# A trunk step with product-key experts on one core: every expert slot handled alone, long work cut into even pieces, six then nine row buffers

## The reference, cut to what matters

```python
def one(hb):                                        # hb: 128 tokens x 1024
    q = (hb @ w_pq).reshape(t, 8, 2, 128)
    sc = jnp.einsum('thpd,hpkd->thpk', q, keys)     # 128 keys per half
    sv, si = lax.top_k(sc, 16)
    cand = sv[:, :, 0, :, None] + sv[:, :, 1, None, :]
    cidx = si[:, :, 0, :, None] * 128 + si[:, :, 1, None, :]
    cv, ci = lax.top_k(cand, 16)
    eidx = take_along_axis(cidx, ci)                # 8 heads x 16 experts per token
    gate = softmax(cv)
    act = gelu(einsum('thkd,td->thk', u_tab[eidx], hb))
    return einsum('thk,thkd->td', gate * act, v_tab[eidx])
```

## Time and profile before

| | us |
|---|---|
| median of 3 runs | 7569.1 (7564.6 to 7570.45) |
| profiled execution, its own time | 7554.87 |
| its span, first to last instruction | 7553.1 |
| PE busy | 4377.6 (58%) |
| DVE busy | 3105.2 (41%) |
| ACT busy | 1460.9 (19%) |
| POOL busy | 1477.2 (20%) |

### The profile page before, as it was taken

How to read it: one execution, slowest core, us unless ns; L and a number is a source line. 1 busy time by engine, 2 the same in 40 slices (tenths; PEclk the granted TensorE clock), 3 DMA queues, 4 the chain that set the end, 5 groups by cost and what they waited for, 6 DMA issues and landing times.

```text
span 7553.1 us, 59355 instructions
## 1 busy us (share of the span) xinstructions
PE 4377.6 (58%) x18966; PEld 1902.7 (25%) x18966; DVE 3105.2 (41%) x7579; ACT 1460.9 (19%) x4806; POOL 1477.2 (20%) x1454
## 2 busy tenths in 40 slices
PE   7999726555553256355579996366545523454455
PEld 2576412222221011111135854022212200111111
DVE  1531462223334354645445215522233344555454
ACT  0142011111111122222222421111111111222222
POOL 0200011111111123234322000111111111333333
PEclk9999857877775577767789998677877756766777
DMA  5102335554554489799941023355555445888998
GB/s 191 55 13 85 133 132 198 201 208 181 191 193 165 178 317 384 282 366 358 363 160 55 1 112 130 142 200 205 202 189 186 182 151 204 327 339 308 361 359 326
DMA packets 222742, 1573.73 MB, mean 208 GB/s; under 512 B 25648, under 2 KB 27312, under 8 KB 35040
## 3 DMA queue, kind: packets, MB, share of 16 engines
q0 software_dynamic: 184320, 1342.26, 47.0%
q1 hardware_dynamic: 38112, 227.68, 8.0%
HBM read 1566.56 MB, written 3.28 MB: 208 GB/s over the span
## 4 chain that ended last, share of the span: by engine, by line
PE 37%; DMA 33%; DVE 14%; ACT 6%; issue 6%; POOL 2%; DVEq 1%; ACTq 0%; SPq 0%; POOLq 0%
DMA arena<-in_experts,arena 31%; PE ps L920 16%; PE ps L704 8%; DVE sq L1374 7%; ACT arena L1061 3%; PE ps L825 2%; ACT arena L1054 2%; PE ps L848 2%; POOL arena L682 2%; DMA arena<-in_weights 2%; PE ps L721 2%; PE ps L870 1%; PE ps L838 1%; PE ps L894 1%; ACT arena L1050 1%
## 5 line engine op out<-in xcount | busy, mean ns | idle before, releaser
L920 PE MATMUL ps<-arena 64*64 64x512 f32 x10240 | 1974.6, 902 | 2843.9 <-ACT arena L1061 2842.5
L1374 DVE CUSTOM_DVE_ANT_0 sq<-arena 128x1024 f32<-128x1024 f32 x1280 | 1568.6, 1225 | 2904.2 <-DMA arena<-in_experts,arena 2875.6
L682 POOL DMA_INDIRECT arena<-in_experts,arena x1280 | 1341.2, 1048 | 5500.4 <-PE ps L920 4283.4
L920 PEld LDWEIGHTS ps<-arena 64*64 64x64 f32 x10240 | 516.4, 186 | 4146.4 <-issue 4145.0
L1050 ACT ACTIVATE arena<-arena 128x2 f32<-128x2 f32 x640 | 130.2, 203 | 4670.5 <-DVE arena L1374 4670.5
L704 PE MATMUL ps<-arena 128*128 128x512 f32 (+3 forms) x1920 | 776.6, 561 | 25.7 <-DMA arena<-in_weights 23.8
L704 PEld LDWEIGHTS ps<-arena 128*128 128x128 f32 x1920 | 369.1, 195 | 432.1 <-issue 383.5
L1054 ACT ACTIVATE arena<-arena 128x1 f32<-128x1 f32 x1280 | 425.5, 379 | 46.3 <-issue 2.4
L1061 ACT ACTIVATE arena<-ident,arena 128x128 f32<-128x128 f32 x1280 | 433.3, 385 | 0.0
L894 PE MATMUL ps<-arena 128*128 128x256 f32 (+1 forms) x1024 | 321.1, 471 | 79.3 <-ACT arena L1026 62.0
L1267 DVE TENSOR_REDUCE negm<-ps 128x1 f32<-128x768 f32 (+4 forms) x160 | 119.0, 745 | 381.2 <-PE ps L831 214.8
(11 more groups left out here) (148 smaller groups left out, 3182.0 us busy)
## 6 DMA issues: line engine op xcount, KB each, us to landing
arena<-in_weights SPq DMA_DIRECT2D x182, 1024.0 KB, 6.8
arena<-in_experts,arena POOLq DMA_INDIRECT x1280, 7.9
arena<-mod_rows SPq DMA_DIRECT2D x24, 512.0 KB, 8.7
arena<-in_weights SPq DMA_DIRECT2D x8, 576.0 KB, 4.7
arena<-in_weights SPq DMA_DIRECT2D x4, 768.0 KB, 4.8
arena<-in_weights SPq DMA_DIRECT2D x6, 512.0 KB, 4.7
x<-in_x_sample SPq DMA_DIRECT2D x4, 512.0 KB, 11.3
arena<-in_g_norm SPq DMA_DIRECT2D x4, 512.0 KB, 11.0
```

Source lines behind the costliest of these rows:

```text
L682: pool.indirect_dma_start(out=ring[BUF[n]], out_offset=None, in_=ins["experts"], in_offset=bass.IndirectOffsetOnAxis(ap=index[n // SLOTS % ...
L920: last = MM(acc[h][to:to + 64, c * 512:(c + 1) * 512], diag[(n + odd) % 4][lo:lo + 64, lo:lo + 64], ring[BUF[n + odd]][lo:lo + 64, D + c * ...
L1374: V.tensor_tensor_reduce(out=sq[:], in0=ring[BUF[n]][:, 0:D], in1=h2_of_slot(n), scale=1.0, scalar=0.0, op0=ALU.mult, op1=ALU.add, accum_o ...
```

## The change

- Slots go one at a time: item `E` is one dot product on DVE; `Ea` is all of ACT's part (one gelu activation, times gate, diagonal), with no return to DVE; `Emm` is the four matmuls of one slot. The slot's gate carries no factor 0.5 now.
- The order is made by `Line`: slot s has its dot at place s, `Ea` at s + 0.4 and `Emm` at s + 1.6; other items are spread by cost over ranges of slots. `g`, `o` and `pq` are cut into 4 pieces, `p` into 2, `tk1` into one per tile, `tk2` into 6 (`tkx` and `tkg` once per tile, except tile 0).
- Buffers: five for the first 20 slots of a layer, six up to slot 259, nine for the last 380. One of them is `front`, where gains, mask and rope lie; SP reloads these for layer 1 after slot 636 of layer 0, and layer 1's `scale1`/`shift1` rows stand behind them in SP's queue.

```diff
-    return [("tk2", l, t, u), ("tkx", l, t, u), ("tkg", l, t, u)]
+    s = [("tk2", l, t, u, j) for j in range(6)]
+    return s + ([("tkx", l, t, u), ("tkg", l, t, u)] if alone else [])
...
+def pieces(items):
+    s = []
+    for i in items:
+        n = {"g": 4, "o": 4, "p": 2, "pq": 4}.get(i[0], 1)
+        s += [("part", i, j, n) for j in range(n - 1)] + [i]
+    return s
...
+    def slots(self, l):
+        n = l * NT * SLOTS
+        for s in range(NT * SLOTS):
+            self.put(s, [("E", n + s)])
+            self.put(s + .4, [("Ea", n + s)])
+            self.put(s + LAG, [("Emm", n + s)])
...
+        line.spread(-2, 16, pieces(r[at:]))
+        line.spread(20, 110, choose(l, 1))
+        line.spread(16, 232, pieces(merge(l, 1) + route(l, 1)))
+        line.spread(232, 250, choose(l, 2))
+        line.spread(262, 330, choose(l, 3))
+        if l == 0:
+            line.spread(300, 560, mod_items(1))
+        line.spread(390, 460, choose(l, 4))
...
-NBUF = 8
+NBUF = 9
...
+for _l in range(L):
+    BUF += [s % 5 for s in range(20)]
+    BUF += [s % 6 for s in range(236)]
+    BUF += [(s + 2) % 6 for s in range(4)]
+    BUF += [(s + 6) % 9 for s in range(380)]
...
                     if l:
-                        sp.wait_ge(*ready("oT", 0, NT - 1, 1))
-                        sp.wait_ge(*ready("qcN", 0, NT - 1))
-                        sp.wait_ge(ob_ready, NT)
-                    sp.dma_start(gains[:], to_all(row("gains", l))).then_inc(consts_in, 16)
+                        sp.wait_ge(slot_used, FINAL_IN[0, 4] + 1)
+                        sp.dma_start(mask, ins["mask"]).then_inc(masks_in, 16)
+                        sp.dma_start(rope, ins["rope"]).then_inc(masks_in, 16)
+                    sp.dma_start(gains, to_all(row("gains", l))).then_inc(consts_in, 16)
...
                     for c in range(2):
-                        for odd in range(2):
-                            for h in range(2):
-                                lo, to = 64 * h, 64 * (h ^ odd)
-                                last = MM(acc[h][to:to + 64, c * 512:(c + 1) * 512], diag[(n + odd) % 4][lo:lo + 64, lo:lo + 64],
-                                          ring[BUF[n + odd]][lo:lo + 64, D + c * 512:D + (c + 1) * 512], start=s == 0, stop=s == SLOTS - 2)
-                    last.then_inc(slot_used, 2)
+                        for h in range(2):
+                            lo, to = 64 * h, 64 * (h ^ (n % 2))
+                            last = MM(acc[h][to:to + 64, c * 512:(c + 1) * 512], diag[n % 4][lo:lo + 64, lo:lo + 64],
+                                      ring[BUF[n]][lo:lo + 64, D + c * 512:D + (c + 1) * 512], start=s < 2, stop=s >= SLOTS - 2)
+                    last.then_inc(slot_used, 1)
...
+                elif kind == "Ea":
+                    n = item[1]
+                    c, s = n % 16, n % SLOTS
+                    act.wait_ge(dot_done, n + 1)
+                    A(gel[:, c:c + 1], dots[:, c:c + 1], ACT.Gelu_apprx_tanh)
+                    act.drain()
+                    A(wts[:, c:c + 1], gel[:, c:c + 1], ACT.Copy, scale=gate[n // SLOTS % 2][:, s:s + 1])
+                    act.drain()
+                    if n >= 4:
+                        act.wait_ge(slot_used, n - 3)
+                    A(diag[n % 4], ident[:], ACT.Copy, scale=wts[:, c:c + 1]).then_inc(diag_done, 1)
```

More of the change, by code:

```diff
@@ L181, in mod_items @@
     return s
-GRP = 2
-NGRP = SLOTS // GRP
 ETILES = [(l, t) for l in range(L) for t in range(NT)]
-def tensor_cost(item):
-    k = item[0]
[L192 to L197, removed]
-    def __init__(self):
[L202 to L252, removed]
@@ L256, with cost @@
-SEAM = 6
+def pieces(items):
[4 more added lines that the diff above has]
+    return s
+def cost(item):
+    k = item[0]
+    if k == "part":
+        k, n = item[1][0], len(GROUPS[item[1][2]]) if item[1][0] == "pq" else 1
+    else:
+        n = len(GROUPS[item[2]]) if k in ("pq", "sc") else 1
+    return {"mod": 7.0, "hT2": 1.2, "g": 1.76, "p": 1.76, "mT": 1.2, "o": 1.76, "pq": .5 * n, "sc": .25 * n,
+            "n2": 3.0, "tk2": 1.5, "tk1": 1.0}.get(k, 0.1)
@@ new lines, with put, spread, items @@
+class Line:
+    def __init__(self):
+        self.points = []
+    def put(self, at, items):
+        self.points += [(at, i) for i in items]
+    def spread(self, a, b, items):
+        total = sum(cost(i) for i in items)
+        at = 0.0
+        for i in items:
+            at += cost(i)
+            self.points.append((a + (b - a) * at / total, i))
+    def slots(self, l):
[4 more added lines that the diff above has]
+            self.put(s + LAG, [("Emm", n + s)])
+        for t in range(NT):
+            end = (t + 1) * SLOTS - 1 + LAG
+            self.put(end + .1, [("ea", l, t), ("ex", l, t)])
+            after = [("sw", l, t, 0), ("sw", l, t, 1), ("ew", l, t)] + ([("g2", l, 1)] if t == 0 else []) + ([("y", t)] if l == L - 1 else [])
+            self.put(end + 2.1, after)
+    def items(self):
+        return [i for _, i in sorted(self.points, key=lambda p: p[0])]
@@ L412 @@
     if _e >= 2:
-        assert PLACE[("tk2", _l, _t, 0)] > PLACE[("Emm", NGRP * (_e - 1) - 1)]
-    for _u in range(4):
-        assert PLACE[("tkg", _l, _t, _u)] < PLACE[("E", NGRP * _e + 16 * _u)]
+        assert PLACE[("tk2", _l, _t, 0, 0)] > PLACE[("Emm", SLOTS * (_e - 1) - 1)]
+    assert PLACE[("tkg", _l, _t, 0)] < PLACE[("E", SLOTS * _e)]
+    if _t == 0:
+        for _u in range(4):
+            assert PLACE[("tkg", _l, _t, _u)] < PLACE[("E", SLOTS * _e + 32 * _u)]
 def build(nc, ins, outs):
@@ L510, in build @@
         esum = take(8)
-        dots, dsq, dlin, dth, dgate, wts = (take(8) for _ in range(6))
+        dots, gel, wts = (take(16) for _ in range(3))
         assert _e[0] <= R0 + 22928
@@ L699, in weight, with project @@
                 return block_in(b)
-            def project(dst, lhs, blocks, cols):
-                for k in range(DK):
+            def project(dst, lhs, blocks, cols, steps):
+                for k in steps:
                     w = weight(blocks[k // 4]).rearrange("p (k n) -> p k n", k=4)
@@ L711, in _ @@
                 if item in BANK:
-                    for before in BEFORE[item]:
-                        pe.wait_ge(*ready(*before))
+                    if piece == 0:
+                        for before in BEFORE[item]:
+                            pe.wait_ge(*ready(*before))
                     dst = psum(item)
-                done = lambda op: op.then_inc(full_sem[kind], 1)
+                done = lambda op: op.then_inc(full_sem[kind], 1) if piece == count - 1 else op
+                steps = lambda n: range(piece * n // count, (piece + 1) * n // count)
                 blocks = blocks_of(item)
@@ L862, in _ @@
                     bc, t = item[2:]
[L863 removed]
+                    done(project(dst, hT(t), blocks, 512, steps(DK)))
                 elif kind == "p":
@@ L1371, in _ @@
-                    c = n0 % 8
-                    for n in range(n0, n0 + GRP):
-                        dve.wait_ge(row_land[BUF[n]], 16 * TURN_OF[n])
-                        V.tensor_tensor_reduce(out=sq[:], in0=ring[BUF[n]][:, 0:D], in1=h2_of_slot(n), scale=1.0, scalar=0.0,
-                                               op0=ALU.mult, op1=ALU.add, accum_out=dots[:, n % 8:n % 8 + 1]).then_inc(dot_done, 1)
-                        dve.drain()
-                    s = n0 % SLOTS
-                    TT(dgate[:, c:c + GRP], dots[:, c:c + GRP], gate[n0 // SLOTS % 2][:, s:s + GRP], ALU.mult)
+                    n = item[1]
```

190 lines of the change are left out of this document (94 added, 96 removed).

## The result

The changed kernel takes 5710.9 us (median of 3, 5710.1 to 5716.2) against 7569.1 us: a ratio of 0.7548, 95% interval 0.7531 to 0.7565, a quarter less time. The profiled execution has a span of 5708.3 us against 7553.1. All times are of undisturbed executions; one of the four with `LAG` 2.6 in experiment 7 ran in a slower state (7608 us, granted clock 0.49) and is left out.

The account below looks back on a forecast made before the run. Stage A was taken as bound by its chain of waits over five buffers, stage B by DMA. 7554.9 - 1321 - 190 + 10 = 6054 us profiled, 6070 us as a median, range 5860 to 6510.

Parts of the forecast that it names:

- stage A: First 256 slots of a layer: 1020 us forecast against 1671 and 1690, 1321 us less over both layers.
- DVE's uneven choices: Choices crowded among slots 232 to 250 and the first 18 of a layer: 50 us added to PE's 970.
- The lap: Gather-to-gather chain in stage A: 12.7 us for two slots before; 16 to 19.6 us per single slot after.
- the price of a slot in stage B: DMA time per 1.049 MB slot: 2.90 us before, 2.75 with queue never idle, 2.83 forecast.
- stage B: Other 384 slots of a layer, bound by DMA: 1160 and 1092 us forecast against 1247 and 1195, 190 less.
- the rest: Norms, attention and first merge, outside both stages: 1750 us, which the change hardly touches.
- The added costs: 26 table loads on ACT (bounds 0 and 33 us) and the layer seam (0 and 15): 10 us more together.
- The seam: Between layers, SP's reload and row loads wait for slot 636: 22 us of cover, cost bounds 0 and 15.
- Rival 1: The order itself stalls stage A: laps up to 29 us, 4.85 us per slot, 6510 us in all; chance 0.24.
- Rival 2: Neighbouring slots overlap on PE: 1.62 us per slot, 5820 us in all; chance 0.13.
- Rival 3: PE's clock stays at 1.2 GHz with half the array used: 3.69 us per slot, about 8050 us; chance 0.02.
- Rival 4: The change doesn't break the lap in stage A, only stage B gains: about 7380 us; chance 0.03.

Follow-up runs that it names:

- experiment 7: Changed kernel, matmuls of two slots issued together on PE, buffers freed in twos: 5535.4 us; with `LAG` (slots behind the odd dot) 1.1, 2.1, 2.6: 5622.3, 5477.0, 5471.8 us.
- experiment 3: Kernel before, with only a pair's weights moved ahead of the next pair's dots on DVE: 6277.2 us, ratio 0.8289.
- experiment 6: Changed kernel with six or four buffers for a layer's last 380 slots, or nine freed in twos: 5747.6, 6214.2, 5724.7 us.

## Why the prediction was wrong, point by point

**The direction and the mechanism of stage A were right, its size in part by luck.** The forecast was 1020 us for a stage; it is 1017 and 1015. The sum had PE busy for 970 us, at 2.30 us per slot, and 50 us for DVE's uneven choices. Measured are 895 us busy, at 1.98 per slot (the lower end of the sum was 880), and 122 us idle: 75 us too much and 72 us too little, which cancel. The clock is 0.96, PE's share 0.88, as foreseen. The lap was read rightly from the earlier trace rows, and experiment 3 shows it by itself.

**The step that failed is the price of a slot in stage B.** I took 2.90 us as today's price, 2.75 "were the queue never idle" and 2.83 as forecast. It is 2.49 (2.52 over stage B of layer 1, 966 / 384). The step rested on the DMA share: 94.9% in the earlier trace rows was read as a queue that is 95% full, so that only 5% were left to gain. The share is no such measure. The gathers' queue of the changed kernel, 2600 to 2900 us (packets, MB, share):

```profile
q0 software_dynamic: 16545, 120.46, 96.6%
```

By this row a packet takes 0.966 x 16 x 300 us / 16545 = 280 ns; by the earlier trace rows it took 0.949 x 16 x 450 / 22269 = 307 ns (estimates from the rows). So an engine counts as busy while its packets are slower. With everything counted the share rose only from 0.95 to 1.01, the rate from 360 to 421 GB/s. A finer view of the kernel before could have warned: its slices between 3500 and 3840 us (experiment 6) reach 429 GB/s beside others at 269, while those of the earlier trace rows end at 406. This step explains (1160 + 1092) - (1024 + 971) = 257 of the 344 us between 6054 and the 5710 of the profiled execution. By the Trainium skill ("DMA: Bandwidth & Descriptors", Specifications) the HBM limit is about 358 GB/s for each core, a stack's 716 divided between two cores; this kernel runs on one core, and 417 GB/s over the 1024 us of stage B lie above that share. Whether it would hold with the second core at work no run here shows. The Trainium skill's same table has a fabric ceiling of 435 GB/s, to which 421 comes near.

**The cut of the stretches.** Stage A was taken to begin at 936 and 4659 us; the first dots are at 892.5 and 4636. 67 us of old stage A were thus booked under "the rest", which the change was said not to touch. With both mended the sum would have been 6054 - 257 - 67 = 5730, within 0.4% of the 5710 measured; that it comes so close rests on the luck in stage A.

**The added costs.** I took 10 us. The seam cost nothing: 780 us from the last slot to the first dot of layer 1, before 782. SP's loads after slot 636 in the changed kernel, and the first use:

```profile
2925.24 0.33 SPq L584 DMA_DIRECT2D front<-in_mask  x1
...
2929.18 1.42 SPq L611 DMA_DIRECT2D arena<-in_g_norm  x1
```

```profile
2946.69 2.36 DVE L1224 SCALAR_TENSOR_TENSOR arena<-arena 128x1024 f32<-128x1024 f32 x2
```

DVE gets to them 14 us after the last slot's end, before 15 (3868.07, where `ea` began at 3852.97 by the timeline). The last row load lands 10.1 us after its issue at 2929.18, 7 us ahead of that use, so the cover was enough. The table loads lie beside other work. One of them in the changed kernel:

```profile
959.41 0.23 ACT L1049 ACTIVATE arena<-arena 128x32 f32<-128x32 f32 x1 [7.55 <-DVEq L1368]
959.66 1.28 ACT L1062 ACT_TABLE_LOAD   x1
960.96 0.20 ACT L1062 ACTIVATE arena<-arena 128x1 f32<-128x1 f32 x1
```

The activation follows 0.02 us after the load ends: each costs 1.28 us. The trace has 34 loads (16 at L1062, 14 at L1049, four elsewhere), not 31, and 5 before: 29 more, 37 us on ACT and not 33. The Trainium skill ("ScalarE: Activation LUTs", What ACT_TABLE_LOAD costs) counts 2.66 us for a switch; the part beyond the load does not show in this trace: the instruction before this load ends 0.02 us ahead of it.

**The rivals.** Rival 1 (stalls) did not come: stage A is 4.0 us per slot. Rival 2 (neighbours overlap on PE) is not seen in stage A: a slot takes 1.98 us in the mean, and in the chain above a piece stands between any two. Where nothing stands between (2500.66 us, 24 records in 4.66 us instead of 3 x 1.95), slots do overlap in part. Its time, 5820, is 2% from the measured one, but for another reason. Rival 3: the clock did not fall with half the array in use, it is 0.97 and 0.98 in stage B, where it was 0.73 and 0.70 before. Rival 4 is refuted.

**The range.** It reached down to 5860. How that end follows is not written out, but with 2.75 us as the floor of a slot stage B could have gained only 768 x 0.08 = 61 us more than forecast; it gained 257 more. A bound that rests on one reading of a share is not a bound.

## What to carry to other kernels

When a ring of buffers feeds in-order engines, count for each buffer what must have landed before it is given back; one item behind the wrong neighbour was worth 1290 us here, more than the added buffers alone (1197). Read a DMA plateau by its GB/s against the best slices of the same trace, not by its busy share, and count the gathers in flight: about four of 1 MB were enough, three were not. After a change that makes one engine the bound, look at what the change made dearer on that engine: here the matmuls of a lone slot, which in pairs gave another 3%, and 4% with a later place.

## What the runs showed of the hardware that I had not expected

- Indirect gathers of 8 KB rows, with some weight loads, hold 417 GB/s over a millisecond and 421 in most slices. With fewer in flight (estimates) the rate was 409 with about 4, 360 with about 3 and 336 with about 2.5, at mean busy shares of 1.00, 0.95 and 0.91.
- Between matmuls in quarters of the array and full-array ones no gap shows in the trace (1399.44 + 1.86, then 1401.30), though they alternate at every slot.
